# Input projection of a gated convolution by seven products of half blocks in place of eight

## What is computed

```python
def short_conv_mixer(h, conv_buf, w_in, w_conv, w_out):
    b_g, c_g, v, z = jnp.split(h @ w_in, 4, axis=-1)
    u = c_g * v
    ...                       # three taps along the tokens
    y = b_g * conv * jax.nn.silu(z)
    return y @ w_out, padded[:, -(CONV_WIDTH - 1):]
```

## Time and profile before

| | us |
|---|---|
| three runs | 2307.36, 2308.59, 2310.74 (median 2308.59) |
| profiled execution, its own time | 2311.37 |
| its span, first to last instruction | 2309.4 |
| mean granted clock of TensorE | 0.974 |
| prologue, with the first tiles of c, v and z | 0 to about 124 |
| conv loop, input projection | about 124 to 975 |
| output projection of the convolution | from about 980 |

### The profile page before, as it was taken

One profiled execution on the slowest core, in us unless ns is written; L12 is line 12 of the kernel. 1 busy time (PEld: TensorE's weight loads), 2 busy tenths in 40 slices (PEclk: granted clock), 3 DMA queues, 4 the chain that ended last, 5 costly groups with the idle time before them and its releaser, 6 DMA issues.

```text
span 2309.4 us, 42465 instructions
## 1 busy us (share of the span) xinstructions
PE 2177.4 (94%) x17176; PEld 2027.1 (88%) x17176; DVE 663.1 (29%) x1161; ACT 595.8 (26%) x879; POOL 674.4 (29%) x287
## 2 busy tenths in 40 slices
PE   7899999999999999999979799997999989989993
PEld 5799999999999999899979799997788865569993
DVE  3412211111111112232247811006443332232226
ACT  3121111111111111222234523322444321122221
POOL 0123333333333333333323233332222200004334
PEclk9999999999999999999989899999999999999997
DMA  9954444444444444322213222225222367752222
GB/s 370 405 186 146 145 145 145 145 147 161 158 161 154 156 153 145 125 73 82 84 58 115 96 73 82 82 82 187 72 71 76 93 195 217 237 176 86 86 81 83
DMA packets 98627, 319.65 MB, mean 138 GB/s; under 512 B 10962, under 2 KB 11090, under 8 KB 97682
## 3 DMA queue, kind: packets, MB, share of 16 engines
q1 hardware_dynamic: 98578, 318.97, 40.3%
HBM read 303.82 MB, written 15.11 MB: 138 GB/s over the span
## 4 chain that ended last, share of the span: by engine, by line
issue 57%; PE 24%; POOL 12%; DVE 2%; SPq 2%; DMA 1%; POOLq 1%; ACT 0%; DVEq 0%; ACTq 0%
POOL w_lo L450 12%; PE ps L498 6%; PE ps L505 3%; PE ps L672 2%; PE ps L687 2%; PE ps L801 2%; PE ps L703 2%; PE ps L832 1%; PE ps L760 1%; SPq L380 1%; SPq L383 1%; PE ps L748 1%; PE ps L716 1%; DVE tiles L1280 1%; DVE x_residual L1274 1%
## 5 line engine op out<-in xcount | busy, mean ns | idle before, releaser
L450 POOL TENSOR_TENSOR w_lo<-w_raw,w_hi 128x1024 fp32r<-128x1024 f32 (+1 forms) x273 | 655.5, 2401 | 1605.8 <-ACT w_hi L881 1605.8
L498 PE MATMUL ps<-operand_hi,w_hi 128*128 128x288 f32 x3680 | 1001.5, 299 | 23.8 <-DVE operand_lo L1175 18.9
L498 PE MATMUL ps<-operand_lo,w_hi 128*128 128x288 f32 x3680 | 997.0, 297 | 0.0
L498 PEld LDWEIGHTS ps<-operand_hi,w_hi 128*128 128x128 f32 x3680 | 695.6, 189 | 33.1 <-issue 23.8
L498 PEld LDWEIGHTS ps<-operand_lo,w_hi 128*128 128x128 f32 x3680 | 694.9, 189 | 0.1
L881 ACT ACTIVATE w_hi<-w_raw 128x1024 fp32r<-128x1024 f32 (+1 forms) x273 | 287.7, 1054 | 1246.6 <-PE ps L505 757.9
L505 PE MATMUL ps<-operand_hi,w_lo 128*128 128x288 f32 x3680 | 524.6, 295 | 0.0
L505 PEld LDWEIGHTS ps<-operand_hi,w_lo 128*128 128x128 f32 x3680 | 500.6, 188 | 0.0
L1254 DVE TENSOR_TENSOR acc<-acc,tmp 128x576 f32<-128x576 f32 x32 | 77.7, 2427 | 303.4 <-ACT tmp L943 303.4
L1122 DVE TENSOR_SCALAR u_sample<-small 128x16 f32 x16 | 4.5, 278 | 367.7 <-PE ps L505 360.9
L537 PE MATMUL ps<-ada_ring,small 128*32 128x128 f32 x2560 | 84.6, 280 | 11.4 <-DMA ada_ring<-adastream 11.4
(11 more groups left out here) (211 smaller groups left out, 2039.6 us busy)
## 6 DMA issues: line engine op xcount, KB each, us to landing
w_raw<-wstream SPq DMA_DIRECT2D x265, 512.0 KB, 3.4
ada_ring<-adastream SPq DMA_DIRECT2D x160, 512.0 KB, 5.8
ada_first_ring<-adastream SPq DMA_DIRECT2D x32, 512.0 KB, 8.1
page_t<-pages SPq DMA_DIRECT2D x48, 320.0 KB, 3.4
page_latent<-pages SPq DMA_DIRECT2D x56, 256.0 KB, 3.0
page_t_end<-pages SPq DMA_DIRECT2D x16, 320.0 KB, 3.4
x_residual<-x_in SPq DMA_DIRECT2D x4, 1152.0 KB, 10.3
x_park<-x_residual SPq DMA_DIRECT2D x1, 4608.0 KB, 16.1
```

Of the source, the lines that this page charges most:

```text
L450: pool.tensor_tensor(WL[:, n.slot, 0:width], WR[:, n.slot, 0:width], WH[:, n.slot, 0:width].bitcast(F32), ALU.subtract).then_inc(w_lo_read ...
L498: pe.matmul(PS[0:cols, 2 * p + a, 0:HALF], WH[:, c.slot, kk * cols:(kk + 1) * cols], x[:, k * T + a * HALF:k * T + (a + 1) * HALF], start= ...
```

## The change

Two output tiles are made together as a 2x2 block product, by seven products in place of eight. Let A be the weights of the two tiles, `A_tq` with t the tile and q the half of the inner dimension (eight blocks of 128), and B the activations, `B_qa` with a the half of the tokens. The kernel computes on the activations once, in place in the buffer of `x`: T1 = B12 - B11, T2 = B22 - T1, T3 = B22 - B12, and B21 - T2, each split into hi (`t_hi`, in the buffer of `tiles`) and lo (`t_lo`, over `x`). For each unit of two tiles VectorE makes from the four raw chunks S1 = A21 + A22, S3 = A11 - A21, S2 = S1 - A11, S4 = A12 - S2. The products, in TensorE's order:

| index | weights | activations | PSUM |
|---|---|---|---|
| 0 | A11 | B11 | bank a |
| 1 | S1 | T1 | bank c |
| 2 | S2 | T2 | bank b |
| 3 | A12 | B21 | added to bank a: first output quarter done |
| 4 | S3 | T3 | added to bank b |
| 5 | S4 | B22 | added to bank c |
| 6 | A22 | B21 - T2 | added to bank b |

A product has 24 matmuls (16 by hi weights, 8 by lo). ScalarE copies bank a after product 0 and bank c after product 1, and VectorE makes the other three quarters by additions from banks b and c between the products. A unit is 168 matmuls for two tiles (192 before), and 31 units with a prologue of two tiles in place of three make 5400 matmuls of 288 columns where 6144 stood.

What moves with it:

- VectorE makes the seven `w_lo` of each unit; GpSimd rests from the prologue's end to the output projection.
- The modulation's pieces go one by one: after products 1, 3, 5 and 6 of each unit. Their ring has six buffers in the prologue and two in the loop.
- SP loads the four chunks of the next unit into four buffers, each as it comes free, between the modulation's pieces.
- `y` of each block goes to HBM (`y_park`) and comes back as four quarters: three during the last unit, the last one after the last gate. `x` is read again from its input (4608 KB) as the output projection begins.

The diff, cut to its core:

```diff
 CH3 = 2 * 3 * P
+CH2 = 2 * 2 * P
+HK = KT // 2
+PROD = 7
+UNITS = 2 * KT - 1
+RING = 6
...
 
 W_THREE = KT // 2
-W_CONV = W_THREE + 2
-W_COUT = W_CONV + 8 * (KT - 1)
+W_PRE = KT // 2
+W_COUT = W_PRE + PROD * UNITS
+S_COUT = W_PRE + 4 * UNITS
+PART_TURNS = 16 * (W_PRE // 2)
 W_KV = W_COUT + KT * 2
 W_MLA = W_KV + W_THREE + 2 + 1
...
+            def load_mod(m, j):
+
+
+                sp.wait_ge(ada_used, m * 8 + (8 * ADA0 - 1 + j))
+                blk = m * 2 + (2 * ADA0 + j // 4)
+                load_ada(blk, j % 4, ADA6[j % 2], ada_landed[j % 2])
+
+            def park_y(m):
+                sp.wait_ge(gate_done, m + 1)
+                for a in range(2):
+                    sp.dma_start(y_park[:, bass.ds(m * T + a * HALF, HALF)], Y[a][:, :]).then_inc(y_parked, 16)
+
+            def unit_loads(m, u):
+                unit = 2 * m + u
+                load_mod(m, 4 * u + 2)
+                sp.wait_ge(part_sums, summed(unit, 4))
+                load_part(unit + 1, 0, RA11, raw_landed[0])
+                load_mod(m, 4 * u + 3)
+                sp.wait_ge(w_lo_ready, operand(m, u, 4).at(1))
+                load_part(unit + 1, 2, RA21[:, :], a21_landed)
+                sp.wait_ge(w_lo_ready, operand(m, u, 5).at(1))
+                load_part(unit + 1, 1, RA12, raw_landed[1])
+                load_mod(m, 4 * u + 4)
+                sp.wait_ge(w_lo_ready, operand(m, u, 6).at(1))
+                load_part(unit + 1, 3, RA22[:, :], a22_landed)
+                load_mod(m, 4 * u + 5)
+
+            for j in range(2):
+                load_mod(0, j)
+
...
+            for q, (idx, j) in enumerate(((1, 4), (2, 5), (4, 6))):
+                load_mod(m, j)
+                sp.wait_ge(w_used, operand(m, 0, idx).at(1))
+                sp.dma_start(B1[:, 4 * q * T:4 * (q + 1) * T], y_park[:, 4 * q * T:4 * (q + 1) * T]).then_inc(x_landed[q], 16)
+            load_mod(m, 7)
+            load_w(Chunk(W_COUT))
+            load_w(Chunk(W_COUT + 1))
+            park_y(m)
+            sp.wait_ge(y_parked, 32 * KT)
+            sp.dma_start(B1[:, 12 * T:], y_park[:, 12 * T:]).then_inc(x_landed[3], 16)
+            sp.wait_ge(w_used, W_COUT)
+            sp.dma_start(X[:, :], x_in).then_inc(x1_back, 16)
+            sp.wait_ge(w_lo_ready, W_COUT)
             sp.wait_ge(ada_used, 8 * (ADA0 + KT))
             sp.dma_start(COS[:, :], cos_in).then_inc(rope_landed, 16)
             sp.dma_start(SIN[:, :], sin_in).then_inc(rope_landed, 16)
...
+            def product(c, hi, lo, bank, first, last):
+
+                pe.wait_ge(w_hi_ready, c.at(1))
+                for k in range(HK):
+                    for x in (hi, lo):
+                        pe.matmul(PS[:, bank, 0:HALF], WH[:, c.slot, k * P:(k + 1) * P], x(k),
+                                  start=(first and k == 0 and x is hi), stop=False, skip_group_check=True)
+                pe.wait_ge(w_lo_ready, c.at(1))
+                for k in range(HK):
+                    done = pe.matmul(PS[:, bank, 0:HALF], WL[:, c.slot, k * P:(k + 1) * P], hi(k),
+                                     start=False, stop=(last and k == HK - 1), skip_group_check=True)
+                done.then_inc(w_used, 1)
...
+            def unit(m, u, mods):
+
+                n = 2 * m + u
+                a, b, c = (0, 1, 2) if u else (3, 4, 5)
+
+                def modulation(slot):
+                    for j in mods[slot]:
+                        if j == 0:
+                            pe.wait_ge(ada_turned, m + ADA0)
+                        ada_chunk(j, j % 2, m * 4 + (j // 2 + 1 + -(-(8 * ADA0 - j % 2) // RING)), 6)
+
+                if u:
+                    pe.wait_ge(u_done, m + 1)
+                else:
+                    wait(pe, z_ready, m)
+                product(operand(m, u, 0), *B11, a, True, False)
+                modulation(0)
+                wait(pe, part_evac, evacuated(n - 2, "c12"))
+                if u and isinstance(m, int) and m == 0:
+                    pe.wait_ge(pre_copied, 1)
+                pe.wait_ge(t_hi, 1)
+                pe.wait_ge(t_lo, 3)
+                product(operand(m, u, 1), *T_1, c, True, False)
+                modulation(1)
+                wait(pe, part_evac, evacuated(n - 2, "c21"))
+                pe.wait_ge(t_hi, 3)
+                pe.wait_ge(t_lo, 4)
+                product(operand(m, u, 2), *T_2, b, True, False)
+                modulation(2)
+                pe.wait_ge(part_copied, copied_to(n, "p1"))
+                product(operand(m, u, 3), *B21, a, False, True)
+                modulation(3)
+                pe.wait_ge(part_evac, evacuated(n, "u2"))
+                pe.wait_ge(t_hi, 4)
+                pe.wait_ge(t_lo, 5)
+                product(operand(m, u, 4), *T_3, b, False, False)
+                modulation(4)
+                pe.wait_ge(part_copied, copied_to(n, "p5"))
+                product(operand(m, u, 5), *B22, c, False, True)
+                modulation(5)
+                pe.wait_ge(part_evac, evacuated(n, "u3"))
+                pe.wait_ge(t_hi, 5)
+                pe.wait_ge(t_lo, 6)
+                product(operand(m, u, 6), *T_4, b, False, True)
+                modulation(6)
...
+            def conv_units(m):
+                unit(m, 0, [(), (0,), (), (1,), (), (2,), (3,)])
+                unit(m, 1, [(), (4,), (), (5,), (), (6,), (7,)])
+
+            conv_units(0)
+            with pe.Fori(1, KT - 1) as m:
+                conv_units(m)
+            unit(KT - 1, 0, [(0,), (1,), (2,), (3,), (4,), (5,), (6, 7)])
...
+            def round_part(c, raw, ready, count):
+
+                act.wait_ge(ready, count)
+                act.wait_ge(w_used, c.at(-1))
+                act.activation(WH[:, c.slot, :], raw, ACT.Copy).then_inc(w_hi_ready, 1)
...
+            def unit(m, u, first=False, last=False):
+
+                n = 2 * m + u
+                v = 0 if u == 0 else 1
+                a, b, c = (0, 1, 2) if u else (3, 4, 5)
+                round_part(operand(m, u, 1), RS1[:, :], part_sums, summed(n, 1))
...
+                round_part(operand(m, u, 2), RA11, part_sums, summed(n, 2))
+                act.wait_ge(w_used, operand(m, u, 0).at(1))
...
+                    act.wait_ge(ada_used, 8 * ADA0)
+                    mixed_hi(2, 0, 1, 5)
+                round_part(operand(m, u, 3), RA12, raw_landed[1], n * 16 + (PART_TURNS + 16))
...
+                if first:
+                    mixed_hi(3, 1, 0, 7)
+                round_part(operand(m, u, 4), RA21[:, :], part_sums, summed(n, 3))
+                round_part(operand(m, u, 5), RA12, part_sums, summed(n, 4))
+                round_part(operand(m, u, 6), RA22[:, :], a22_landed, n * 16 + 16)
+                if not last:
+                    round_part(operand(m, u, 7), RA11, raw_landed[0], n * 16 + (PART_TURNS + 32))
...
+            def mix_rest(lo):
+
+                dve.wait_ge(h_ready, lo + HK + HK // 2)
+                mix((0, 1), (1, 1), (0, 1), lo, HK // 2)
+                mix((1, 1), (1, 1), (0, 0), lo, HK // 2)
+                mix((1, 0), (1, 0), (1, 1), lo, HK // 2)
...
+            def part_sum(out, x, y, op, *ready):
+
+                for s, value in ready:
+                    dve.wait_ge(s, value)
+                dve.tensor_tensor(out, x, y, op).then_inc(part_sums, 1)
+
+            def part_lo(c, raw):
+
+                dve.wait_ge(w_hi_ready, c.at(1))
+                dve.tensor_tensor(WL[:, c.slot, :], raw, WH[:, c.slot, :].bitcast(F32), ALU.subtract).then_inc(w_lo_ready, 1)
...
+            def unit(m, u, consume, last=False, first=False):
+
+
+                n, v = 2 * m + u, u
+                b, c = (1, 2) if u else (4, 5)
+                part_lo(operand(m, u, 1), RS1[:, :])
+                part_sum(RA21[:, :], RA11, RA21[:, :], ALU.subtract, (raw_landed[0], n * 16 + (PART_TURNS + 16)), (part_sums, summed(n, 1)))
+                part_sum(RA11, RS1[:, :], RA11, ALU.subtract, (part_sums, summed(n, 3)), (w_lo_ready, operand(m, u, 1).at(1)))
+                if first:
+                    mixed_lo(1, 1, 1, 3, 7, HK // 2)
+                part_lo(operand(m, u, 2), RA11)
+                consume(1)
+                part_lo(operand(m, u, 3), RA12)
+                part_sum(RA12, RA12, RA11, ALU.subtract, (part_sums, summed(n, 2)), (w_lo_ready, operand(m, u, 3).at(1)))
+                if first:
...
+                    wait(dve, z_ready, m)
+                dve.tensor_tensor(C12[v][:, :], PS[:, b, 0:HALF], P1[v][:, :], ALU.add).then_inc(part_evac, 1)
+                part_lo(operand(m, u, 4), RA21[:, :])
+                if first:
+                    mixed_lo(3, 1, 0, 5, 7, 0, HK)
...
+                dve.tensor_tensor(C22[v][:, :], PS[:, b, 0:HALF], P1[v][:, :], ALU.add).then_inc(part_evac, 1)
+                part_lo(operand(m, u, 6), RA22[:, :])
+                dve.wait_ge(part_evac, evacuated(n, "u3"))
+                dve.wait_ge(part_copied, copied_to(n, "p5"))
```

(44 more changed lines are left out.)

349 lines of the change are left out of this document (222 added, 127 removed).

## The result

The changed kernel took 2323.97 us (median of 4 runs, 2320.69 to 2326.37), the kernel before 2307.98 in the same session (4 runs). The ratio is 1.0065, 95% interval 1.0053 to 1.0077: **slower by 0.65%**, small but clear of the noise, where 0.6% faster was forecast. The profiled execution took 2325.15 us with a span of 2323.3. The forecast for it was 2297.1: it took 28 us more.

A forecast was written before the change was run, and what follows sets the result against it. TensorE, busy 94% of the span, was taken as the bound, with a hidden chain binding once relieved. An output projection 16.6 us earlier, less 2.3 lost to x's reload, turned 2311.4 into 2297.1 us profiled (2294.3 against runs); range 2246 to 2332.

The forecast's parts named there:

- end of product 5 of unit 0: Start of the loop: VectorE's extra work leads to 147.3 us, and the first unit's product 5 ends at 148.4.
- 29 units: Loop after the first unit: each unit takes 26.59 us, against 27.69 for its two tiles before.
- last unit: End of the loop, a piece after each product: 13.09, five products 16.1 and four pieces 2.48, to 951.2 us.
- end of product 6 to output projection: After the loop: gate, parks, y's last quarter and first low part put TensorE's start 12.05 us later, at 963.2.
- second tile's weights late: Output projection: weights queued behind x's reload are rounded at 30 us, wanted at 27.7; loss 2.3 us.
- Six ring buffers: Prologue: six buffers still exceed what TensorE leaves waiting during one group's 24 matmuls (3.2 us), so its pace is kept.
- The chain: Loop, product 5 through A22's load, S1, S3, S2 to next product 2: 13.09 us, TensorE waiting 1.57 per unit; chance 0.45.
- the first rival: Loop: TensorE stays the bound, the chain being shorter by 1.57 us per unit; 47 us less, 2247; chance 0.15.
- The gate: Between the last product and the output projection: the gate's operations take about 2.9 us.
- The longer chain: Rival, loop: slower landings and waits add 0.9 us per unit, 26 us more, 2320; slower from 0.5 us; chance 0.22.
- The clock: Rival, units: clock drops at the wait before product 2, 1.6 us per unit, 46 us in all, 2340; chance 0.13.
- That combination: Rival: change fails its purpose, or start and tail cost ten more than summed; within a few us of before; chance 0.05.

The follow-up runs named there:

- experiment 3: Changed kernel with eight ring buffers in place of six for the prologue's first 48 modulation pieces: 2315.59 us, ratio 1.0023 to the kernel before.
- experiment 1: Changed kernel with the next unit's A22 load issued ahead of the modulation load it stood behind: 2278.52 us, ratio 0.9861 to the kernel before.
- experiment 2: Changed kernel with silu ahead of the rounding of the output projection's first weights on ScalarE: 2314.97 us, ratio 1.0019 to the kernel before.
- experiment 4: Changed kernel with A22's load moved ahead, silu before the weights' rounding and eight prologue buffers together: 2260.09 us, ratio 0.9788 to the kernel before.
- experiments 6: On top of experiment 4, VectorE waits for y's quarters one by one, not for the last before its first low part: 2263.55 us, ratio 0.9785.
- experiment 7: On top of experiments 6, unit 0's A21 and A22 asked behind the ring's last piece, S1 made behind the mixes: 2259.14 us, ratio 0.9779.
- experiment 8: On top of experiment 7, one weight chunk of the output projection's second tile asked ahead of x's reload: 2257.38 us, ratio 0.9776.
- experiment 5: Changed kernel with A22's load moved behind one more modulation load: 2477.87 us, ratio 1.0719 to the kernel before.
- experiment 9: On top of experiment 8, the output projection's first two weight chunks and last modulation piece asked ahead of y's third quarter: 2256.92 us, ratio 0.9776.

## Why the prediction was wrong, and where it was right

From 2297.1 to the 2325.15 us measured, by its own steps:

| step | forecast | measured | us |
|---|---|---|---|
| end of product 5 of unit 0 | 148.4 | 157.2 | +8.8 |
| 29 units | 26.59 each | 27.01 each | +12.3 |
| last unit | 31.67 | 32.3 | +0.6 |
| end of product 6 to output projection | 12.05 | 20.8 | +8.8 |
| second tile's weights late | 2.3 | 0 | -2.3 |

The sum of the last column is 28.2, so 2325.3.

- **"Six ring buffers are still more than TensorE leaves waiting ... so I keep the prologue's pace" failed.** It was argued from one group's 24 matmuls (3.2 us) alone. With six the last turn comes 9.1 us later, and experiment 3, with eight, returns 8.5 of it. Why six are too few is argued: TensorE's longest stretches on other work leave more waiting than they hold, and the first fill is a quarter smaller. What followed the prologue was right: from the eighth turn to the end of product 5 are 35.0 us here (122.2 to 157.2), and 35.3 in the forecast (113.1 to 148.4). There a slip helped a little: the forecast's own terms add up to 28.1 us and 146.9, not 147.3.
- **The chain was right in every link and its owner was right**, as experiment 1 shows by removing it. TensorE waited for the two roundings, 0.87 us at a time. It was sized 0.42 us too short per unit, and the largest part is the landing: 4.1 and 0.13 to be seen, where 29 landings show 4.40 (3.93 to 5.19). That is 0.17 per unit. Behind it, from S1's start to the end of S2's rounding, 7.44 us stand on average where 7.33 was taken (0.11): in every second unit the modulation's turn and VectorE's own loop turn lie in the chain, and it is 7.71 in place of 7.22. From product 2 to the next piece behind product 5, where no wait is left, TensorE takes 13.69 where 13.58 was taken (0.11), and A22's request comes 1.41 after the piece's start and not 1.38 (0.03). These parts are read from the trace; no run took one of them away by itself. "Each 0.1 us in the chain is 3 us of the whole" held.
- TensorE's own work in a unit is 25.35 us, not 25.02 (experiment 1). A change of shape costs both the piece and the product after it: 0.57 for a piece and 0.11 more on the product's first matmul, 0.68 where I took 0.62, and 0.03 for each product's boundary. Under the chain only 0.11 of this came through; it made the first rival's 2247 too low by 10 us.
- **The gate, "about 2.9", failed.** It took 12.1 us in the changed kernel and 2.5 in experiment 2. The forecast counted the gate's operations and did not ask what stands on ScalarE ahead of silu. That was a wait for a load which stands in the queue behind the reloads of y, which this change had added. Experiment 2 removed 8.0 us of it. With it gone, the step is 13.0 us in experiment 4, where 12.05 was forecast.
- The loss of 2.3 for x's reload did not appear because the reload was priced too high. It landed at 1003.9, 11.3 us behind the last quarter of y (992.6) and not 14.2; the second tile's first chunk landed at 1007.0, 19.7 us after that quarter's request (forecast 22.9), and was rounded 1 us before TensorE wanted it at 1009.1:

```profile
1007.05 1.06 ACT L1049 ACTIVATE w_hi<-w_raw 128x1024 fp32r<-128x1024 f32 x1 [12.00 <-DMA w_raw<-wstream]
```

In experiments 2 and 4, where TensorE came earlier but still behind the last quarter, no such wait appeared either. It appeared as 1.3 and 2.0 us when TensorE no longer waited for that quarter (experiments 6 and 7), and went when one chunk was asked ahead (experiment 8).
- **The rivals.** TensorE as the bound was wrong for the kernel as given, though one swapped pair of loads makes it true, at 2278 rather than 2247 since prologue and gate still lose. The Trainium skill, Perfetto Trace Analysis, section "Identifying the Most-Contended Engine", says to optimize the engine with the highest occupancy first; that its relief should arrive in full was the forecast's own reading of this. Here TensorE's 51 us less of busy time came with a span 14 us longer. The longer chain had its sign right: 0.42 us a unit longer, under the 0.5 from which I said it decides. Alone it would have left a gain; it took prologue and gate, 17.6 us together, to turn it. That combination I had priced at ten us and given 0.05. The clock did not fall: 1.00 in the units, with gaps of up to 1.3 us in most of them. Its price was also too high: two windows with 10 matmuls in place of 15 are 1.3 us and not 1.6, and in experiment 5, where the clock did fall, 0.9 a unit came through.
- VectorE was to be busy for 70 to 80%; the window gives 486.85 of 730, 67%. Its order did not bind.

The errors of size lie on the same side. Two of them, 17.6 of the 28 us, are of one kind: a resource that the change made scarcer (ring buffers; the place of the output projection's weights in the DMA queue, and with it ScalarE's order) was costed at what it had been before. The third, 12.3 us, is a chain whose links were each a little short, paid 29 times.

## What to carry to other kernels

When work is taken off the bounding engine, write down the chain that it hid, and look for the first load in it: here a load stood behind another load for whose buffer SP waited, and swapping the two was worth 45 us of the span, three times what the whole change lost. Where a change shrinks a ring or adds transfers, follow each queue's order by hand past the new entries, and every engine's order for what now stands behind a wait. A small operation of VectorE that meets GpSimd's element-wise work should be priced at that work's duration, not at its own.

The change itself pays once its loads are in order: 2256.9 to 2260.1 us (experiments 4 and 7 to 9), 2.1 to 2.2% faster than the kernel before, each within the others' intervals.

## What the runs showed of the hardware

- VectorE's two-input operations were held to GpSimd's pace in three places: 2.02 and 2.48 us for 288 columns in place of 0.46 (changed kernel), up to 2.92 for 576 columns in place of 0.75 (experiment 7), 2.61 and 2.48 when the same GpSimd work was moved over the gate (experiment 9). Each of these ended a fixed time behind the GpSimd low part beside it, 0.3 us for 288 columns and 0.6 for 576. GpSimd's low parts took 2.3 to 2.9 us themselves.
- Gaps of TensorE of 1.3 us left the granted clock at 1.00 over 730 us; gaps of 4.1 to 5.3 us, once a unit, brought it to 0.92 over the same stretch, with 0.50 in the two us shown after one. Where between them it turns, no run shows.
- A 512-KB load as second of two was seen 4.15 us after its issue in the unit shown and 4.40 on average; with none just ahead of it, 3.34 and 3.43 (experiment 1).
- S2 waits on VectorE for S3, the operation just before it, and started 0.03 us after its end (437.31 behind 436.06 + 1.22), where the forecast took 0.16.
